# Two fused transformer blocks on one core: the second output projection by token halves, with the norm, the router and the row tiles of the first half inside it

## The reference

```python
# first block
x = x + rmsnorm(mixed @ w_out, attn_post_norm)                   # first output projection
h = rmsnorm(x, ffn_pre_norm)
u = causal_depthwise_conv(h @ w_up, conv_w, conv_b)
gate, up = split(u, 2)
x = x + rmsnorm((gelu(gate) * up) @ w_down, ffn_post_norm)
# second block
hc = modulate(rmsnorm_2(ctx, g_mix), csh1, csc1)                 # 256 context tokens
h = modulate(rmsnorm_2(x, g_mix), sh1, sc1)
q, k, v, bg, cg, hv = split(h @ w_in_2)
x = x + gt1 * (concat([att, conv]) @ w_out_2)                    # second output projection
h2 = modulate(rmsnorm_2(x, g_ffn), sh2, sc2)
aff = softmax(h2 @ w_router)                                     # 16 experts
g, idx = top_k(aff.T, 128)                                       # each expert takes 128 tokens
x = x + gt2 * segment_sum(expert(h2[idx]) * g)
return rmsnorm_2(x, g_final)
```

## Time and profile before

| | us |
|---|---|
| three runs, lowest / median / highest | 2700.7 / 2703.43 / 2704.67 |
| the profiled execution | 2702.21 |
| its span, first to last instruction | 2700.4 |
| PE busy in the span | 2508.4 (93%) |
| DVE, ACT, POOL busy | 1626.8, 1166.4, 675.3 |
| mean granted TensorE clock | 0.965 |

### The profile page before, as it was taken

The page is one execution under the profiler, slowest core; times in us unless marked ns, Lnnn a source line. Parts: engine busy times, 40 slices in busy tenths (PEclk is TensorE's granted clock), DMA queues, the critical chain, the costliest instruction groups (busy, mean ns, idle before and its releaser), DMA issues.

```text
span 2700.4 us, 34356 instructions
## 1 busy us (share of the span) xinstructions
PE 2508.4 (93%) x11874; PEld 1985.7 (74%) x11874; DVE 1626.8 (60%) x2499; ACT 1166.4 (43%) x1711; POOL 675.3 (25%) x401
## 2 busy tenths in 40 slices
PE   5999899978899989989989899999987899999996
PEld 2886467767678877777778678788864588888885
DVE  4122696656453346574542534488427899999997
ACT  4021353343443322343333421244223588888886
POOL 0211110013344467334456322410110011111100
PEclk9999899989899999899999899999988799999998
DMA  6010000022222254222222211100023999999995
GB/s 271 28 35 16 32 1 1 0 78 78 67 90 93 95 188 174 72 78 94 93 104 99 78 63 47 47 1 0 16 79 126 398 381 396 396 396 396 396 394 211
DMA packets 85913, 378.86 MB, mean 140 GB/s; under 512 B 7916, under 2 KB 9116, under 8 KB 71456
## 3 DMA queue, kind: packets, MB, share of 16 engines
q1 hardware_dynamic: 81072, 360.26, 35.2%
q0 software_dynamic: 4752, 17.43, 2.4%
HBM read 356.60 MB, written 21.05 MB: 140 GB/s over the span
## 4 chain that ended last, share of the span: by engine, by line
PE 65%; issue 16%; DVE 7%; POOL 7%; ACT 3%; DMA 1%; POOLq 0%; ACTq 0%; SPq 0%; DVEq 0%
PE ps L854 7%; PE ps L856 7%; PE ps L855 7%; PE ps L1110 6%; PE ps L1112 6%; PE ps L1111 6%; POOL w_lo L2168 5%; PE ps L687 5%; PE ps L679 3%; PE ps L824 2%; POOL a_lo L2172 2%; PE ps L744 2%; PE ps L746 2%; PE ps L745 2%; PE ps L1020 1%
## 5 line engine op out<-in xcount | busy, mean ns | idle before, releaser
L2168 POOL TENSOR_TENSOR w_lo<-arena,w_hi 128x1024 fp32r<-128x1024 f32 x180 | 438.3, 2436 | 804.8 <-ACT w_hi L1313 804.7
L2055 DVE TENSOR_TENSOR e_lo<-arena,e_hi 128x1024 fp32r<-128x1024 f32 x384 | 453.2, 1221 | 35.8 <-ACT e_hi L1536 23.2
L1536 ACT ACTIVATE e_hi<-arena 128x1024 fp32r<-128x1024 f32 x384 | 403.9, 1061 | 102.5 <-PE ps L1112 102.5
L854 PE MATMUL ps<-h_hi,w_hi 128*128 128x512 f32 x848 | 340.9, 402 | 32.3 <-POOL w_lo L2168 19.9
L1313 ACT ACTIVATE w_hi<-arena 128x1024 fp32r<-128x1024 f32 x180 | 189.8, 1055 | 398.9 <-PE ps L856 398.9
L856 PE MATMUL ps<-h_hi,w_lo 128*128 128x512 f32 x848 | 334.7, 395 | 0.0
L855 PE MATMUL ps<-h_lo,w_hi 128*128 128x512 f32 x848 | 334.6, 395 | 0.0
L854 PEld LDWEIGHTS ps<-h_hi,w_hi 128*128 128x128 f32 x848 | 162.0, 191 | 76.2 <-issue 30.6
L1110 PE MATMUL ps<-e_hi,x_hi 128*128 128x512 f32 x512 | 202.9, 396 | 4.0 <-DVE e_lo L2055 4.0
L1853 DVE SCALAR_TENSOR_TENSOR arena<-ps,cols,arena 128x511 f32<-128x511 f32 x88 | 63.8, 746 | 232.8 <-ACT arena L1378 232.8
L1112 PE MATMUL ps<-e_lo,x_hi 128*128 128x512 f32 x512 | 200.0, 391 | 0.0
(11 more groups left out here) (314 smaller groups left out, 4821.7 us busy)
## 6 DMA issues: line engine op xcount, KB each, us to landing
arena<-in_w_up SPq DMA_DIRECT2D x108, 1024.0 KB, 8.3
arena<-in_w_down SPq DMA_DIRECT2D x86, 1024.0 KB, 8.2
arena<-in_w_gate SPq DMA_DIRECT2D x64, 1024.0 KB, 9.8
arena<-in_w_in SPq DMA_DIRECT2D x18, 1024.0 KB, 4.8
arena<-in_w_ada SPq DMA_DIRECT2D x12, 1024.0 KB, 12.8
arena<-in_w_out SPq DMA_DIRECT2D x12, 1024.0 KB, 4.8
arena<-in_w_ada SPq DMA_DIRECT2D x24, 512.0 KB, 6.7
routed_rows<-arena SPq DMA_DIRECT2D x8, 520.0 KB, 2.6
```

Of the source, the lines that this page charges most:

```text
L854: pe.matmul(out, w_hi[:, q, w], hi, start=start, stop=False)
L1536: act_e.activation(e_hi[:, (2 * sl + a) % RING, :], slot[sl][:, a * D:(a + 1) * D], ACT.Copy).then_inc(s_ehi, 1)
L2055: v.tensor_tensor(e_lo[:, r, :], slot[sl][:, a * D:(a + 1) * D], e_hi[:, r, :].bitcast(F32), ALU.subtract).then_inc(s_elo, 1)
L2168: gp.tensor_tensor(w_lo[:, q, :], slot[c][:, q * D:(q + 1) * D], w_hi[:, q, :].bitcast(F32), ALU.subtract).then_inc(s_wlo, 1)
```

## The change

The second output projection becomes sixteen parts like the first: eight for the first token half, then eight for the second. Each of the four weight groups is loaded twice and each part split twice (eight loads of 1 MB in place of four, sixteen high and low parts in place of eight). VectorE adds all parts to the residual; GpSimd only splits weights. Norm 12 becomes norm 12 (first half) and 13 (second half), 512 columns each. Into the second eight parts go norm 12, eight row tiles (four of x, four of `hT`, all through one pair of PSUM banks, so each `row_turn` waits for ScalarE's copy of the one before), the router products of the first half and their softmax. Behind the pass come norm 13, two row tiles ahead of its spread, the second half's router products, softmax and the other row tiles. VectorE's addition of gate2 to its bias moves behind the second expert's count, and SP stores rows 1 to 7 ahead of the gate2 weight loads.

In seam 1 ScalarE copies out all parts from the ninth on, VectorE's branch additions alternate with the sums of norm 4, mean 3 stays, spread 3 moves one k forward, mean 4 moves from part 12, k = 7 to part 13, k = 2, and spread 4 with it to k = 7. In seam 2 TensorE also waits for ScalarE's copies of the down result before its first input part; mean 9 goes into that part, mean 10 two k back, spread 9 into the second part, mean 11 from k = 1 to k = 7 of the sixth part, spread 11 behind the context key products. ScalarE's root 9, with its table load, and a weight split go into the squares of norm 10; VectorE scales all eight context tiles ahead of the branch, and alternates branch additions with the sums of norm 11.

The core of the diff (TensorE, seams 1 to 3):

```diff
             output_part(KT, {5: lambda: mean(3)})
-            output_part(KT + 1, {2: lambda: spread(3)})
-            for i in range(2, 4):
+            output_part(KT + 1, {1: lambda: spread(3)})
+            for i in range(2, 5):
                 output_part(KT + i)
-            output_part(KT + 4, {7: lambda: mean(4)})
-            output_part(KT + 5, {4: lambda: spread(4)})
+            output_part(KT + 5, {2: lambda: mean(4), 7: lambda: spread(4)})
             for i in range(6, KT):
                 output_part(KT + i)
...
-            input_half(0, 0)
-
+            pe.wait_ge(eva, T_IA - 2)
+            input_half(0, 0, {1: lambda: mean(9)})
+            pe.wait_ge(evv, T_IA)
             pe.wait_ge(eva, T_IA)
-            mean(9)
-            pe.wait_ge(evv, T_IA)
-            input_half(0, 1, {4: lambda: mean(10)})
-            input_half(0, 2, {0: lambda: spread(9), 2: lambda: spread(10)})
+            input_half(0, 1, {2: lambda: spread(9), 6: lambda: mean(10)})
+            input_half(0, 2, {3: lambda: spread(10)})
             input_half(0, 3)
             input_half(0, 4)
-            input_half(0, 5, {1: lambda: mean(11), 6: lambda: spread(11)})
+            input_half(0, 5, {7: lambda: mean(11)})
...
             i.then_inc(s_cx, 1)
+            spread(11)
...
+            def output_part2(i, between={}):
+                t, h, half = T_OUT2 + i // 2, i % 2, i // KT
...
+                pe.wait_ge(s_wlo, 2 * G_OUT2 + i + 1)
...
+            def row_turn(j):
+
+                h, t = row_tile(j)
+                src, bank = (hT if h else xT), (4 if j < 8 else 2 * (j % 2))
+                if j < 8 or j >= 10:
+                    pe.wait_ge(s_rte, j if j <= 8 else j - 1)
+                for k in range(KT):
+                    m = pe.transpose(ps[:, bank + k // 4, (k % 4) * P:(k % 4 + 1) * P], src[:, k, t * P:(t + 1) * P], ident)
+                m.then_inc(s_rtp, 1)
...
+            for i in range(KT):
+                output_part2(i)
+            output_part2(KT, {4: lambda: mean(12)})
+            output_part2(KT + 1, {2: lambda: spread(12)})
+            for i in range(2):
+                output_part2(KT + 2 + i, {1: lambda: row_turn(2 * i), 5: lambda: row_turn(2 * i + 1)})
+            output_part2(KT + 4, {0: lambda: logits(0), 6: lambda: logit_rows(0)})
+            output_part2(KT + 5, {5: lambda: row_turn(4)})
+            output_part2(KT + 6, {1: lambda: row_turn(5), 5: lambda: row_turn(6)})
+            output_part2(KT + 7, {1: lambda: row_turn(7)})
+            mean(13)
+            pe.wait_ge(evv, T_OUT2 + 8)
+            pe.wait_ge(eva, T_OUT2 + 8)
+            row_turn(8)
+            row_turn(9)
+            spread(13)
+            logits(1)
+            row_turn(10)
+            logit_rows(1)
+            row_turn(11)
```

ScalarE, seams 1 and 2 in part, and seam 3:

```diff
-                if i % 2:
-                    odd_part(i)
-                output_high(i + 2)
+                if i >= KT or i % 2:
+                    even_or_odd_part(i)
+                if i != KT - 1:
+                    output_high(i + 2)
...
-            squares(10, lambda k: yT[:, k, :], lambda k: [(evv, d), (eva, d)])
-            input_high(2)
-            root(9)
+            squares(10, lambda k: yT[:, k, :], lambda k: [(evv, d), (eva, d)], {3: lambda: root(9), 6: lambda: input_high(2)})
+            spread(9)
...
+            squares(12, lambda k: xT[:, k, lo], gated, {k: (lambda k=k: output2_high(k + 1)) for k in range(1, KT)})
+            output2_high(KT + 1)
+            root(12)
+            output2_high(KT + 2)
+            spread(12)
+            shift_half(0, range(4))
+            output2_high(KT + 3)
+            shift_half(0, range(4, KT))
+            squares(13, lambda k: xT[:, k, hi], lambda k: gated(KT + k),
+                    {1: lambda: (row_out(0), row_out(1), output2_high(KT + 4)), 2: lambda: (row_out(2), row_out(3), output2_high(KT + 5)),
+                     3: lambda: (logits_copied(0), router_exp(0), output2_high(KT + 6)), 4: lambda: (row_out(4), output2_high(KT + 7)),
+                     5: lambda: (row_out(5), row_out(6)), 6: lambda: row_out(7)})
+            root(13)
+            row_out(8)
+            row_out(9)
+            spread(13)
+            shift_half(1, range(KT))
+            logits_copied(1)
+            row_out(10)
+            router_exp(1)
+            for j in range(11, 2 * NT):
+                row_out(j)
```

VectorE, seams 1, 2 and 3:

```diff
-            branch_added(0, zT[0], "attn_post", rs, range(5), lo)
-            even_part(KT + 2)
-            branch_added(0, zT[0], "attn_post", rs, range(5, KT), lo)
-            sums(4)
+            branch_added(0, zT[0], "attn_post", rs, range(2), lo)
+            sums(4, {k: (lambda k=k: branch_added(0, zT[0], "attn_post", rs, range(k + 1, min(k + 2, KT)), lo)) for k in range(1, KT)})
...
+            context_scaled(range(KT))
...
+                    part0(T_IA + 1, q2[:, 0, lo], HD ** -0.5)
+                branch_added(3 * KT, yT, "ffn_post", rs, range(k + 1, min(k + 2, KT)), hi)
+            sums(11, {k: (lambda k=k: branch_rest(k)) for k in range(1, KT)})
...
+            gated(0)
+            sums(12, {k: (lambda k=k: gated(k)) for k in range(1, KT)})
+            diagonal(12)
+            gated(KT)
+            rs = spread_ready(12)
+            scaled(0, rs, range(4))
+            gated(KT + 1)
+            scaled(0, rs, range(4, KT))
+
+            def second_gated(k):
+                gated(KT + k)
+                if k == 3:
+                    affinity(0)
+            sums(13, {k: (lambda k=k: second_gated(k)) for k in range(2, KT)})
+            scaled(1, inverse(13), range(KT))
+
+            affinity(1)
...
-            v.wait_ge(s_g2, 1)
-            v.wait_ge(s_late, 48)
-            v.tensor_tensor(gt2B, banks(2, D), gt2B, ALU.add).then_inc(s_g2e, 1)
-
             for e in range(NE):
+                if e == 2:
+                    v.wait_ge(s_g2, 1)
+                    v.wait_ge(s_late, 48)
+                    v.tensor_tensor(gt2B, banks(2, D), gt2B, ALU.add).then_inc(s_g2e, 1)
```

249 lines of the change are left out of this document (117 added, 132 removed).

## The result

| | before | after |
|---|---|---|
| median of 19 runs, us | 2705.14 | 2710.05 |
| lowest to highest | 2700.36 to 2707.94 | 2703.75 to 2711.72 |
| profiled execution / its span | 2702.21 / 2700.4 | 2711.66 / 2709.9 |
| mean granted TensorE clock | 0.965 | 0.962 |

The ratio is 1.0017, 95% interval 1.0011 to 1.0024: slower by 4.9 us, clear of noise but within the 0.2% that I had called no change. The forecast was +0.2 and 2703.6; the range to 2712 held the time. In microseconds, 2710.05 lies above the 2698.0 to 2708.9 that I had written for no change, because the median of before is 2705.14 in these runs and was 2703.43 in the three that I had. The two profiled executions lie near the low end of the one kernel's runs and at the top of the other's, so their difference (9.5) is larger than that of the medians. What follows compares stretches.

What follows compares the result with a forecast made beforehand. TensorE was taken as the bound, the expert phase full, so seam changes reach the end. -4.6 - 0.1 + 4.9 = +0.2 on the profiled 2702.2, with the median 1.2 above: 2703.6; range 2690 to 2712.

Steps and rivals of the forecast that it cites:

- The expert phase gives nothing back: Expert phase, TensorE busy 50.00 of 50.00 and DMA share 1.00: what the seams gain or lose reaches the end.
- Seam 1, -4.6: First output projection to up's start: -11.3 of waits gone, +2.0 for mean 4 later, +4.7 new waits; ends -9.3 and 0.
- so up moves with mean 4: First output projection: mean 4 and spread 4 keep their five k of distance, so up's start shifts as mean 4 does.
- Seam 2, -0.1: Start of the second block, to spread 11: 12.3 new against 12.4 gone; ends -5.3 and +5.
- Seam 3, the pass, +21.2: Second output projection: work among matmuls 16.0, wait at row tile 2 3.5, clock behind it 1.7; grows by 21.2.
- Seam 3, behind the pass, 22.8: From the second output projection's end to the search's first copy: 22.8 after against 37.9, a gain of 15.1.
- gate2, -1.2: First count behind the search: less waiting for gate2, its addition coming back later at 1.23; net -1.2.
- The table load: Norm 10's squares and ahead of second exp: 1.28 per load, no drain; by the skill's page two loads would add 2.8.
- Rival A: All three seams: stalls go, nothing replaces them; -9.3, -5.3, -0.3, giving 2688.5; chance 0.33 including what lies up to the forecast.
- Rival B: Second output projection: TensorE waits for ScalarE's copy at row tile 2 and each pair after, price 11; 2714; chance 0.17.
- Rival C: Weight-part waits 5.25 and 6.69 stay because GpSimd holds the low parts; seams 1, 2 at +2, +5; 2715; chance 0.08.

Runs made afterwards that it cites:

- seam 1 alone: Kernel before with only the first output projection's part of the change: 2698.31 against 2705.12, ratio 0.9974.
- kernel with the tiles behind: Changed kernel with all sixteen row tiles behind the pass, in two pairs of PSUM banks: 2694.20, ratio 0.9960 to the kernel before.
- seam 2 alone: Kernel before with only the change at the start of the second block: 2708.06 against 2705.12, ratio 1.0007.
- the mended kernels: Kernel before with seams 1, 3 changed, row tiles behind the pass, splits 12, 13 early: ratio 0.9929; plus seam 2, mean 9 late: 0.9930.

## Why the prediction was right, and where its steps failed

By the medians of the runs with one seam each, the seams give -6.8, +2.9 and +7.7 where I had -4.6, -0.1 and +4.9, so one miss cancels part of the two others. The profiled executions say something else: -1.8, +3.7 and +9.2 (212.4 against 203.2 from the pass's start to the first expert product). By them all three seams came out 3 to 4 us worse than forecast, 11 in sum, and the medians of the whole change differ by less because the profiled execution of before is one of its fast ones and that of after one of its slow ones. So the number was right in part by luck. The direction that the runs can tell, slower by 0.11 to 0.24%, was not in the number. It was given as within 0.2%, and it is.

- **"The expert phase gives nothing back"** held: windows and stretch after are as before, and the seams' changes reach the end.
- **Seam 1, -4.6**: the waits were 1.95 and 2.04 (3.4 and 1.3 forecast), and mean 4 came within 0.4 of its place. The step that failed is "so up moves with mean 4". The distance of five k between mean 4 and spread 4 is not fixed when TensorE is at half clock: 7.00 in place of 4.36. My sum put the clock behind the two new waits at nothing and named it only as one end of the range. The trace has -1.8, the runs of seam 1 alone have -6.8, and my -4.6 lies between. Where half clock is granted varies between executions: the kernel with the tiles behind, whose code is the same up to there, took 111.3. That doesn't explain the -6.8, since most profiles have 115.4; where the rest of it arises stays open.
- **Seam 2, -0.1**: the waits summed to 6.4 of the 6.9 forecast. The trace has +2.1 with seam 2 alone and +3.7 in the changed kernel. The term that was mis-sized is the clock: I took 0.4 for what stands behind five waits. In the changed kernel half the clock stood for 6.85 us behind the first of them, which costs 3.4. And from mean 11 (1541.83) to spread 11 (1548.64) are 6.81, where a mean, a k and the key products at full clock are 0.9 + 0.7 + 3.6 = 5.2. Together that is 5.0 in place of 0.4.
- **Seam 3, the pass, +21.2**: measured +23.4. The wait at row tile 2 was 3.51 for 3.5, at the place and for the reason named. Behind it 2.9 were lost at half clock for 1.7. The work put among the matmuls is 17.0 (104.34 - 87.32) for 16.0.
- **Seam 3, behind the pass, 22.8**: measured 24.8. To the mean 2.49 for 2.6; from the mean's end to the first product 6.8 for 5.0, since the tiles there ran at half clock (3.19 for two, has 1.09 for one); the products 8.72, 1.8 more than 6.9, about the 2 that I gave the clock for the whole stretch; then 5.9 for 5.3.
- **gate2, -1.2**: measured -2.5 and +1.5, -1.0.
- **The table load**: the exponential of the second half starts at once behind its load, in ScalarE's rows after:

```profile
2048.51 1.28 ACT L1553 ACT_TABLE_LOAD   x1
2049.80 0.26 ACT L1553 ACTIVATE tiny<-tiny 128x64 f32<-128x64 f32 x1
```

1.29 lie between the two starts, and the row copy ahead of the load ends at 2048.49, so no gap stands on that side either. By the drain of about 1380 ns that the Trainium skill ("ScalarE: Activation LUTs", "What ACT_TABLE_LOAD costs") counts beside the load, an estimate would have the exponential start 1.4 later. This trace doesn't agree, as the earlier trace rows didn't.
- **Rival A** (the stalls go) didn't come; the mended kernels, at 2684.6 and 2685.2, show that its 2688.5 can be reached, but with other edits. **Rival B** named row tile 2 as the place, as the forecast did. It expected a wait at each pair after it too, because of the one pair of banks; there was one wait, and it came from ScalarE's order. Its sizes, -2, +2 and +11 for the seams, are nearer to the profiled -1.8, +3.7 and +9.2 than mine, and 2710.05 lies between its 2714 and my 2703.6. **Rival C** is excluded, since 5.25 and 6.69 went with the order.

What the prediction had in its hands and didn't use: it wrote that row tiles "lie beneath" the search, where VectorE works 45.9 us alone, and that work among the matmuls costs its full time. Together these say that moving eight tiles into the pass is a loss of 7 us, and that norm and router alone are worth moving, since behind the pass they stand on the path. The kernel with the tiles behind showed both: 7.35 less in the pass without the tiles, and for norm and router 9.7 more in the pass against 16.6 less behind it.

## What to carry to other kernels

Before moving work into a stage that TensorE bounds, ask what covered it where it was. Here norm and router had no cover and gained by moving, and the row tiles lay beneath a search and lost. And count a new wait of TensorE as its length and possibly the half clock behind it, which also stretches any chain that runs through TensorE's next instructions. Here waits of 1.5 to 6.7 us lost a further 1.6 to 3.4 at the places named above; but the 1.95 before part 12 in the changed kernel lost nothing more. The order of one ScalarE instruction was worth 6.4 us of the pass.
